# Two attention out-projections as seven block products: a four-part network on one Trainium2 core

## The reference, cut to what matters

```
# layer 0 (retention)
q, k, v, gate = split(x @ a_w_in)            # 4 heads: q, k 256 wide, v, gate 512 wide
o = normalised(chunkwise_retention(rope(q), rope(k), v))
x = layer_norm(ALPHA * x + (o * silu(gate)) @ a_w_out)   # 2048 -> 1024, called AO below
# layer 1 (latent attention, 16 heads of 128)
c = x @ kv_w_down;  k_nope, v = split(rms(c) @ kv_w_up)
q_lat, gate = split(x @ b_w_in);  q = rms(q_lat) @ b_w_uq
o = causal_softmax_attention(q, k, v)
x = layer_norm(ALPHA * x + (o * silu(gate)) @ b_w_out)   # 2048 -> 1024, called BO below
# layer 2
h = rmsnorm(x)
x = x + concat(pool_mixer(h @ w_in), neighbourhood_attention(h @ w_in)) @ w_out
x = x + square(relu(rmsnorm(x) @ w_up)) @ w_down         # 4096 -> 1024, called DN below
return rmsnorm(x)
```

## Time and profile before

| | |
|---|---|
| times of three runs | 1442.5, 1440.75, 1440.86 us (median 1440.86) |
| profiled execution | 1442.41 us, its span 1440.9 us, mean granted PE clock 0.998 |
| busy of the span: PE, PEld | 1428.7, 1210.5 us |
| busy: DVE, ACT, POOL | 746.8, 610.7, 502.6 us |
| DMA | 192.94 MB, mean 134 GB/s |
| chain that ended last | PE 93%; ACT 2%, DVE 2%, issue 1%, POOL 1% |

### The profile page before, as it was taken

The page is one execution under the profiler, slowest core; times in us unless marked ns, Lnnn a source line. Parts: engine busy times, 40 slices in busy tenths (PEclk is TensorE's granted clock), DMA queues, the critical chain, the costliest instruction groups (busy, mean ns, idle before and its releaser), DMA issues.

```text
span 1440.9 us, 18940 instructions
## 1 busy us (share of the span) xinstructions
PE 1428.7 (99%) x7036; PEld 1210.5 (84%) x7036; DVE 746.8 (52%) x1278; ACT 610.7 (42%) x1011; POOL 502.6 (35%) x225
## 2 busy tenths in 40 slices
PE   9999999999999999999999999999999999999998
PEld 7888888888888888888888888888888888888887
DVE  6344453544561745444545445646865111159896
ACT  4323332332345534443444333558854232254554
POOL 5334342455634332342333225435214444310000
PEclk9999999999999999999999999999999999999999
DMA  7222124725763532323313462243517222355552
GB/s 286 88 96 88 66 90 151 261 87 149 207 166 123 179 109 74 117 76 106 106 58 105 127 254 104 101 153 117 176 62 216 88 87 87 145 158 194 199 189 110
DMA packets 35826, 192.94 MB, mean 134 GB/s; under 512 B 3776, under 2 KB 8512, under 8 KB 16192
## 3 DMA queue, kind: packets, MB, share of 16 engines
q1 hardware_dynamic: 28512, 146.26, 29.1%
q10 hardware_dynamic: 4960, 29.23, 5.8%
q0 software_dynamic: 2304, 16.78, 5.7%
HBM read 184.92 MB, written 40.89 MB: 157 GB/s over the span
## 4 chain that ended last, share of the span: by engine, by line
PE 93%; ACT 2%; DVE 2%; issue 1%; POOL 1%; DMA 0%; ACTq 0%; SPq 0%; DVEq 0%
PE bank L496 26%; PE bank L498 26%; PE bank L497 26%; PE bank L1023 6%; PE bank L985 4%; PE bank L1084 2%; PE bank L1002 1%; PE bank L758 1%; DVE h_tok L1914 0%; PE bank L880 0%; DMA stage<-in_w 0%; POOL wlo L613 0%; PE bank L725 0%; PE bank L728 0%; PE bank L726 0%
## 5 line engine op out<-in xcount | busy, mean ns | idle before, releaser
L613 POOL TENSOR_TENSOR wlo<-stage,whi 128x1024 fp32r<-128x1024 f32 (+1 forms) x178 | 444.3, 2517 | 711.8 <-ACT whi L1310 646.0
L496 PE MATMUL bank<-xhi,whi 128*128 128x512 f32 (+1 forms) x504 | 195.1, 387 | 0.0
L498 PE MATMUL bank<-xhi,wlo 128*128 128x512 f32 (+1 forms) x504 | 194.5, 386 | 0.0
L497 PE MATMUL bank<-xlo,whi 128*128 128x512 f32 (+1 forms) x504 | 194.4, 386 | 0.0
L1310 ACT ACTIVATE whi<-stage 128x1024 fp32r<-128x1024 f32 (+1 forms) x158 | 160.4, 1066 | 69.1 <-PE bank L498 62.4
L498 PEld LDWEIGHTS bank<-xhi,wlo 128*128 128x128 f32 x504 | 94.7, 188 | 19.3
L496 PEld LDWEIGHTS bank<-xhi,whi 128*128 128x128 f32 x504 | 94.7, 188 | 18.8
L497 PEld LDWEIGHTS bank<-xlo,whi 128*128 128x128 f32 x504 | 94.7, 188 | 18.7
L2340 DVE TENSOR_TENSOR hid<-relu 128x512 f32 (+1 forms) x32 | 23.2, 723 | 138.2 <-ACT relu L1778 138.2
L496 PE MATMUL bank<-whi,xhi 128*128 128x512 f32 (+1 forms) x236 | 90.3, 382 | 0.9 <-POOL wlo L613 0.9
L498 PE MATMUL bank<-whi,xlo 128*128 128x512 f32 (+1 forms) x236 | 89.7, 380 | 0.0
(11 more groups left out here) (358 smaller groups left out, 3586.9 us busy)
## 6 DMA issues: line engine op xcount, KB each, us to landing
stage<-in_w SPq DMA_DIRECT2D x99, 1024.0 KB, 4.8
tsum<-in_w POOLq DMA_DIRECT2D x16, 1024.0 KB, 9.9
stage<-tsum SPq DMA_DIRECT2D x16, 1024.0 KB, 4.8
stage<-in_w SPq DMA_DIRECT2D x8, 1152.0 KB, 6.1
tsum<-in_w ACTq DMA_DIRECT2D x8, 1024.0 KB, 18.1
o_spill<-gt SPq DMA_DIRECT2D x16, 256.0 KB, 6.1
bT<-o_spill SPq DMA_DIRECT2D x4, 1024.0 KB, 9.0
xres<-in_x ACTq DMA_DIRECT2D x1, 2048.0 KB, 9.3
```

What stands on the lines that cost most here:

```text
L496: pe.matmul(dst, a_hi, b_hi, start=start, stop=False)
L497: pe.matmul(dst, a_hi, b_lo, start=False, stop=False)
L498: return pe.matmul(dst, a_lo, b_hi, start=False, stop=stop)
L613: pool.tensor_tensor(lo[:, r], stage[p % 2][:, r], hi[:, r].bitcast(F32), ALU.subtract).then_inc(w_lo, 1)
```

## The change

AO and BO are now computed as DN is: seven products of 2 x 2 blocks, each of two steps (`dq` = 2) of four 128-channel blocks, 14 steps of 24 matmuls, 336 each. DN keeps its 28 steps; in all three the products stand in another order. Two of the seven products are copied by ACT from PSUM to SBUF as they end (`keep`), summed there by DVE, and used for three quarters of the output. The gather into the rows is spread over the steps on DVE, and only the last product's rows are gathered at the end, with the row sums. The operand's and the panels' remainders are written by POOL for the first two steps of AO and BO and by DVE for the others.

`tsum` grows from 16 to 32 panels. ACT copies and POOL adds stand in other places: the sums of AO after head 0 and in heads 2 and 3; those of BO around AO and B0; those of DN in the loop over pairs (now at two of six places in it), at L0 and later. The fields of `Seven` are: steps in one product, place among the semaphore counts, first panel, first sum, additions to await before each sum is loaded, and PSUM banks of each product.

```diff
+PLAIN = (0, None, None, None, 1, 3, None)
+SUMMED = (None, 2, 0, 1, None, None, 3)
+Seven = namedtuple("Seven", "dq at w sums ready banks")
+AO = Seven(2, 0, END, 0, (4, 6, 4, 8), ((0, 1), (2, 3), (4, 5), (6, 7), (0, 1), (2, 3), (6, 7)))
...
# SP
+            def seven_load(st, d):
+                f, g = divmod(d, st.dq)
+                if d >= 3:
+                    sp.wait_ge(d_tlo, 2 * (st.at + d - 2))
+                if g == 0 and SUMMED[f] is not None:
+                    sp.wait_ge(t_sum, 16 * st.ready[SUMMED[f]])
+                sp.dma_start(seven_stage(st, d)[:, 0:PAN], seven_panel(st, f, g)).then_inc(d_ld[(st.at + d) % 3], 16)
...
-            load(BO + 1)
+            sp.wait_ge(w_lo, 2 * L0)
+            seven_load(BO, 1)
             sp.wait_ge(m_kv, 4 * PAIRS)
             for c4 in range(4):
                 if c4 == 3:
-                    load(BO + 2)
+                    sp.wait_ge(m_g, 2 * PAIRS + 2)
+                    seven_load(BO, 2)
                     store(PAIRS - 1)
                 for e in range(2):
                     sp.wait_ge(m_st[e], 32 * (c4 + 1) + 16)
                 sp.dma_start(bT[:, 4 * c4:4 * c4 + 4, :], ...
...
+            for d in range(3, 14):
+                seven_load(BO, d)
# POOL
-            with pool.Fori(1, AO // 2) as i:
-                for j in range(2):
-                    split_lo(j, PAN, 2 * i)
-            split_lo(AO)
...
+            for p in range(2, B0):
                 split_lo(p)
-                g = p - (AO + 2)
-                if g < DQ:
-                    add_to_sum(0, g, weight_panel(0, 1, g), 2 * DQ)
-                elif g < 2 * DQ:
-                    add_to_sum(2, g - DQ, weight_panel(1, 1, g - DQ), 2 * DQ)
+                if p in (6, 7):
+                    add_to_sum(AO, 0, p - 6, 2, 4)
+                elif p in (8, 9):
+                    add_to_sum(AO, 2, p - 8, 3, 4)
+                elif p in (14, 15):
+                    add_to_sum(AO, 1, p - 14, 3, 6)
+                elif p in (20, 21):
+                    add_to_sum(AO, 3, p - 20, 1, 8)
+            weights_lo(AO, 0)
+            operand_lo(AO, 0)
+            operand_lo(AO, 1)
+            weights_lo(AO, 1)
+            for g in range(2):
+                add_to_sum(BO, 0, g, 2, 12)
+            for g in range(2):
+                add_to_sum(BO, 2, g, 3, 12)
+            for p in range(B0, M0 - 1):
+                split_lo(p)
+                if p >= B0 + 2:
+                    add_to_sum(BO, 1, p - (B0 + 2), 3, 14)
             split_lo(M0 - 1, PAN_R)
             with pool.Fori(0, PAIRS // 2) as i:
                 for j in range(6):
                     split_lo(M0 + j, PANEL if j % 3 == 0 else PAN, 6 * i)
-                    if j == 3:
-                        pool.wait_ge(t_copy, 16 * (3 * DQ + 1))
...
+                    if j % 3 == 0:
+                        dst, b = ((0, 2), (2, 3))[j // 3]
+                        pool.wait_ge(t_copy, 16 * 25)
...
+            weights_lo(BO, 0)
+            weights_lo(BO, 1)
+            for g in range(2):
+                add_to_sum(BO, 3, g, 1, 16)
             for p in range(L0, L0 + 6):
                 split_lo(p)
+                if p >= L0 + 2:
+                    add_to_sum(DN, 1, p - (L0 + 2), 3, 28)
# PE
+            for d in range(13):
+                f, g = divmod(d, AO.dq)
...
+                seven(AO, d, (0, 1)).then_inc(d_pe, 1)
+            seven(AO, 13, (0,)).then_inc(d_end, 1)
+            turn_x(xres, n_x, 0, 0)
+            seven(AO, 13, (1,)).then_inc(d_pe, 1)
+            turn_x(xres, n_x, 0, 1)
# ACT
+            def keep(st, d):
+                if d in (st.dq + 3, 2 * st.dq + 2):
...
+                    for a in range(2):
+                        copy(kept(st)[:, f, a, :], bank[st.banks[f][a]][:, :], d_x)
...
+            for h in range(HA):
+                head(h, h == HA - 1)
+                if h == 0:
+                    copy_sum(AO, 0, lambda g: block_panel(AO, 0, g))
+                    copy_sum(AO, 2, lambda g: block_panel(AO, 2, g))
...
+            act.dma_start(rows[:, :, :], t["ln"][0]).then_inc(aux["rows"], 16)
+            act.wait_ge(t_sum, 16 * 8)
+            copy_sum(BO, 0, lambda g: block_panel(BO, 0, g))
+            copy_sum(BO, 2, lambda g: block_panel(BO, 2, g))
+            for d in range(2, 14):
...
+                rounded(AO, d)
...
-            act.wait_ge(t_sum, 16 * 2 * DQ)
-            copy_sum(1, lambda g: t["tsum"][0, g, :, :])
+            act.wait_ge(t_sum, 16 * 14)
+            copy_sum(BO, 3, lambda g: sum_panel(BO, 1, g))
+            copy_sum(DN, 0, lambda g: block_panel(DN, 0, g))
+            copy_sum(DN, 2, lambda g: block_panel(DN, 2, g))
             with act.Fori(0, PAIRS // 2 - 1) as it:
                 pairs(it)
...
             act.dma_start(mixT[:, 0:2, :], t["static"]).then_inc(aux["static"], 16)
-            split_hi(L0 + 2, y_done, 4 * TT)
+            act.wait_ge(t_sum, 16 * 24)
+            copy_sum(DN, 1, lambda g: sum_panel(DN, 0, g))
+            split_hi(L0 + 2, d_pe, BO.at + 14)
# DVE
+            for d in range(2, 14):
+                gathers(AO, 0, d)
+                remainders(AO, d)
             dve.wait_ge(aux["rows"], 16)
-            norms(0, ln=0, gb=rows, ...
+            norms(ln=0, gb=rows, ...
```

More of the change, by code:

```diff
@@ L1 @@
+from collections import namedtuple
 from contextlib import ExitStack
@@ L557, in _ @@
                     "k p n -> p k n")).then_inc(bld[c4], 16)
-            with sp.Fori(0, (L0 + 2 - BO) // 2) as i:
-                for j in range(2):
-                    load(BO + 3 + j, PAN, 2 * i)
-            load(L0 + 5)
+            for d in range(3, 14):
+                seven_load(BO, d)
+            for p in range(L0, L0 + 6):
+                if p < L0 + 2:
+                    sp.wait_ge(d_tlo, 2 * (BO.at + 13 + p - L0))
+                load(p)
             def band(hp):
@@ new lines, in seven @@
+            def seven(st, d, blocks, dst=None, c0=0, c1=512, start=False):
+                s_hi, s_lo = operand_parts(st, d)
+                wh, wl = [w.rearrange("p (k n) -> p k n", k=PK) for w in seven_parts(st, d)]
+                f, g = divmod(d, st.dq)
+                pe.wait_ge(d_slo, st.at + d + 1)
+                for kk in range(PK):
+                    if kk % 2 == 0:
+                        pe.wait_ge(d_tlo, 2 * (st.at + d) + kk // 2 + 1)
+                    for a in blocks:
+                        r = slice(a * P, (a + 1) * P)
+                        to = bank[st.banks[f][a]][:, c0:c1] if dst is None else dst
+                        last = split_dots(pe, to, s_hi[:, kk, r], s_lo[:, kk, r], wh[:, kk, c0:c1], wl[:, kk, c0:c1],
+                                          (start or g == 0) and kk == 0, g == st.dq - 1 and kk == PK - 1)
+                return last
@@ L1565, in pairs @@
                     exps(0)
-                    split_hi(p + 3, m_kv, c(4, 4), PANEL, n)
+                    if last and s == 1:
+                        act.wait_ge(m_kv, c(4, 4))
+                        weights_hi(BO, 0)
+                    else:
+                        split_hi(p + 3, m_kv, c(4, 4), PANEL, n)
                     turned(0, 0)
@@ new lines, in operand_lo, with remainders @@
+            def operand_lo(st, d):
+                hi, lo = operand_parts(st, d)
+                dve.wait_ge(d_shi, st.at + d + 1)
+                lo_of(lo, operand(st, d), hi, d_slo)
+            def remainders(st, d):
+                operand_lo(st, d)
+                for b in range(2):
+                    r = slice(b * PAN // 2, (b + 1) * PAN // 2)
+                    dve.wait_ge(d_thi, 2 * (st.at + d) + b + 1)
+                    lo_of(seven_parts(st, d)[1][:, r], seven_stage(st, d)[:, r], seven_parts(st, d)[0][:, r], d_tlo)
+                    if b == 0 and d + 1 < 7 * st.dq:
+                        combine(st, d + 1)
```

689 lines of the change are left out of this document (364 added, 325 removed).

## The result

The changed kernel took 1501.45 us (median of 4 runs, 1499.48 to 1503.43) against 1441.28 us before: the ratio is 1.0416, 95% interval [1.0403, 1.0429]. I had forecast 1473 us within 1453 to 1493: the sign was right, the size was half of what came.

What follows compares the result with a forecast made beforehand. It took PE to bound the kernel, busy for 1428.7 of 1440.9 us. The terms summed to +32.1 us on the profiled 1442.4, giving 1474.5; less 1.5 for the median, 1473 us, range 1453 to 1493.

Steps and rivals of the forecast that it cites:

- a): AO and BO: 96 fewer matmuls on PE, 21.7 us gained.
- b): Head 1: PE stalls for panel 7 while POOL waits for four copies, +8.1 us (5 to 10).
- c): Start of AO: loads slowed among copies to 11.6 us, nearly covered by three open stages; +2 us (0 to 6).
- d): End of AO: tile 0's gather, centre and norm chain is late for the transposes; +2.5 us (1 to 4.5).
- e): Start of the pairs: POOL waits for ten copies, so PE waits for panel M0+1; +26.4 us (20 to 34), largest term.
- f): Start of BO: the fourth step's load, queued behind the last reload of bT, is late; +4.5 us (0 to 12).
- rival C: AO and BO: DVE, 92% busy, falls behind in both projections; 1490 to 1510 us, chance 0.10.
- g): End of BO: same chain as d) plus a root mean square, two panels behind may wait; +4.5 us (1 to 8).
- h): Panel L0+3: POOL's addition waits for four copies of DN's second sum, making the panel late; +5.8 us (1 to 10).
- The same copies at the eighth head step ... stand where they stood: Neighbourhood attention: its eighth-step copies and DN's last sum keep their places; nothing was added to the sum.
- rivals A: Faster: copies land before POOL's waits bind, so b), e) and h) go; about 1424 us, chance 0.07.
- B: Near no change: copies land at 2 us each, e) is 10 us, sum -1; 1433 to 1450 us, chance 0.06.

Runs made afterwards that it cites:

- experiment 2: Changed kernel with POOL's wait for copies and its addition in the loop over pairs behind the third and sixth panel, not first and fourth; 1472.85 us.
- pairs_sixth: all_late with both additions of the loop over pairs behind the sixth panel of a turn; 1433.59 us, 0.9955 of the kernel before.
- Experiments 1: Changed kernel without any copies or additions that build sums of weights, plain quarters loaded instead (output not the reference's); 1434.45 us, 0.9949 of the kernel before.
- 5: Changed kernel with SP loading BO's step 3 right behind step 2, ahead of the last store and reload; 1494.96 us.
- 6: Changed kernel with BO's step 3 loaded early, norm rows, bias table and edge fetched at step 6, POOL's two additions after five PE steps; 1492.83 us.
- all_late: Changed kernel with additions of AO, pairs and DN's second and fourth sums later, BO's step 3 loaded early, its tables and additions later; 1442.1 us.
- experiments 3: Changed kernel with DN's second sum copied at the neighbourhood attention's eighth step, added from WO+2, and its fourth copied at UP's end, added in DN; 1481.87 us.
- 4: Changed kernel with DN's second sum still copied at L0, its additions moved to panels from WO+2 on, fourth sum to UP and DN; 1490.34 us.

## Why the prediction was wrong, step by step

- **a) Matmuls.** Right: AO alone, with its small waits, got 10.2 of 10.9 us shorter.
- **b) Head 1.** Right: the four copies landed at 86.2 + 13.3 = 99.5 (forecast 100.3), POOL stood 27.3 us, the wait was 6.69 (6.7). Beyond it the stretch got 2.4 longer, not 1.4, with the granted clock at 0.50 up to 108 us.
- **c) Start of AO.** Too high by 2. SP's loads there landed in 5.8 to 12.4 us, as crowded as I had assumed, and PE waited for none, since three stages were ahead. The rule of the Trainium skill (DMA: Bandwidth & Descriptors, Queues, rings and completion order), by which queues take turns, gave the right term, 0, and its number fits as well: three loads issued at 334.3, 339.0 and 343.7, beside ACT's copies alone, landed in 9.5, 9.7 and 9.9 us, and twice 4.8 is 9.6. The 11.2 to 11.6 of rows 8 misled me; the load of 12.4 was issued together with one of POOL's additions, in a third queue.
- **d) End of AO.** Too high: 0.3 in place of 2.5, in spite of a slow centring; a chain without the mean square fits.
- **e) Start of the pairs.** Right in mechanism and near in size. The ten copies,

```profile
L1396 ACTq DMA_DIRECT2D tsum<-in_w x8: 611/635/731, 474.1 to 478.9; - x8
L1396 ACTq DMA_DIRECT2D tsum<-tsum x2: 522/563/604, 472.9 to 473.5; - x2
...
DMA to landing us min/median/max: 6.1/18.1/29.4
```

ended at 478.9 + 29.4 = 508.3 (506.3), POOL stood 46.1 us, the wait was 26.4 (24.0 + 1.0), and experiment 2 took all of it away. Beyond the waits 3.5 us were lost in place of 1.4; 0.6 of them are in pairs_sixth too, which has no wait there. After the wait the granted clock stayed at its lower level for 6 us.

```profile
512.00:514.00 2.00, 1.60 (x4) 1.31 (x5) 0.00 (x0) 0.00 (x0) 2.00 (x2) 0.50 0.99 197
...
516.00:518.00 2.00, 2.00 (x6) 1.61 (x5) 0.00 (x0) 0.07 (x1) 2.00 (x2) 0.50 1.01 299
518.00:520.00 2.00, 2.00 (x9) 1.61 (x9) 0.69 (x1) 0.52 (x1) 1.32 (x1) 0.91 0.80 318
```

- **f) Start of BO.** The first step that failed. The place was right (the fourth step's load, behind the reload), the duration not: I took a load among others at 11.6 us and it landed in 18.8. I had named the additions and tables beside it and given them nothing (3.5 of wait and 1.4 of clock are already 4.9, for the 4.5 that I took), when they more than doubled the bytes in flight. The wait alone is 12.3 us. Experiments 1, 5 and 6 show it: 5 us from the sums, the rest from the tables and the place in the queue, which no run separates. PE's wait names DVE's wlo, and for more than 10 us, which I had called the sign of rival C; it is not, for DVE itself stood idle, behind ACT's rounding and the load:

```profile
904.50 1.23 DVE L1923 TENSOR_TENSOR wlo<-stage,whi 128x1024 fp32r<-128x1024 f32 x1 [13.80 <-ACT whi L1358]
```

- **g) End of BO.** 5.1 of wait for the 4.5 forecast, near; but it grows to 8.2 as soon as f) is cured (experiments 6, 7). So the two were one budget, not two terms: DVE is behind, and the long wait in f) let it catch up. It gathers tile 0 2.4 us after its product's last matmul in the changed kernel and 5.6 after it in all_late. That is rival C in part, which I had put at 0.10. I had counted DVE 92% busy; in AO, from 345 to 393 us, it was busy for 47.85 of 48 us (third figure with a bracket), with no wait of PE:

```profile
345.00:393.00 48.00, 48.00 (x213) 39.77 (x212) 47.85 (x54) 29.49 (x32) 3.33 (x4) 1.00 0.94 309
```

- **h) Panel L0+3.** Right: the stretch is 5.6 longer (5.8).
- **What was not in the sum.** "The same copies at the eighth head step ... stand where they stood" looked at which instructions stayed, not at what runs beside them. I had counted POOL's wait at L0+3, and neither the spill of v behind four copies in ACT's queue, nor the band reloads beside POOL's additions: 13.1 us of wait and 16.7 in the ledger, which experiments 3 and 4 explain. This is the second step that failed: h) put the copies and additions at L0 into the sum for the one panel behind POOL's wait, and at nothing for all that runs beside them.

The rivals A and B did not occur; copies took the time that the rows gave. (Two sums in them are off, without effect: A's remaining terms c), d), f) and g) are 13.5, or 11.5 without c), and B adds up to -0.2, not -1.) The net, once no wait for a sum is left, is small: 21.7 us of matmuls went, and 7 to 8 us came out in pairs_sixth; 2.5 of its gain lie behind BO's transposes, where no matmul was removed and where the kernel before has a collision like those above (an h_tok operation of 5.73 us at 1091.34). Of the rest, 12.8 are BO's (84.9 us for the 72.1 that 83.0 less 48 matmuls would be), by the wait for h_tok, DVE's late remainders and the clock.

## What to carry to other kernels

A DMA that builds something ahead of time costs nothing only if nobody stands behind it: list for each copy and addition what is queued behind its wait on its engine, what is behind it in its queue, and which small, urgent DMAs run beside it. When a stall is forecast from a load, add up the bytes in flight at that moment, what stands ahead in the load's own queue and how many other queues are busy, rather than take the landing of a typical crowded load. And two waits that an engine's backlog links are not two terms: cure the first and the second grows.

## What the runs showed of the hardware

One DVE operation on 128x256, 0.35 us in its 15 other executions, took 5.68 us: it began 0.03 us before two POOL operations of 5.48 in all, and ended 0.2 us after the second. The Trainium skill (SBUF — State Buffer, Terms) says that the loser of the port that DVE and GpSimd share is blocked for a whole instruction; here it was shut out over two that followed each other. The same befell other operations: one of 1.28 us took 6.17 when it began 0.08 before such a pair (all_late, 1105.57), and 1.28 when it began 0.6 before it (pairs_sixth). Half a microsecond of timing so decides over some 5 us on DVE, and over 2.2 to 3.4 us of waiting on PE where it stands on the path.

PE's granted clock was 0.50 when it went on after each of the changed kernel's six waits of 5.0 to 26.4 us, and after the 2.25 us of rows 7. Two stretches show what was lost beyond a wait: 2.4 us at head 1 (9.1 less 6.7) and 2.9 to 3.5 in the pairs (30.9 less 26.4 and the 1.0 at panel B0+1, less the 0.6 that stays without the wait).
